# Row projections by halves of k with 512 moving columns, and split output projections

## The reference

```
h = rms_norm(x); a_u, a_v, a_g, b_q, b_k, b_v, b_g, m_q, m_g = split(h @ w_in)      # layer 0
...
h = rms_norm_2(x); q, k, v, g_ret, x_lru, y_lru, gate_ret, gate_lru = split(h @ w_in)   # layer 2
o = head_group_norm(retention(rotary(q), rotary(k), v))
y_a = (o * silu(g_ret)) @ w_ret_o
y_b = (rg_lru(conv(x_lru)) * gelu(y_lru)) @ w_lru_o
x = x + (sigmoid(gate_ret + b0) * y_a + sigmoid(gate_lru + b1) * y_b) @ w_out
h = rms_norm_2(x); gate, val = split(h @ ffn_w_up)
x = x + (gelu(conv(gate)) * val) @ ffn_w_down; return rms_norm_2(x)
```

## Time and profile before

| | us |
|---|---|
| median of 3 runs | 942.85 (942.73 to 944.76) |
| the profiled execution, its own time | 941.22 |
| its span, first to last instruction | 939.4 |

### The profile page before, as it was taken

How to read it: one execution, slowest core, us unless ns; L and a number is a source line. 1 busy time by engine, 2 the same in 40 slices (tenths; PEclk the granted TensorE clock), 3 DMA queues, 4 the chain that set the end, 5 groups by cost and what they waited for, 6 DMA issues and landing times.

```text
span 939.4 us, 15308 instructions
## 1 busy us (share of the span) xinstructions
PE 897.5 (96%) x6134; PEld 826.5 (88%) x6134; DVE 564.0 (60%) x1092; ACT 369.1 (39%) x682; POOL 103.3 (11%) x114
## 2 busy tenths in 40 slices
PE   6999998999999989999999999999999999999996
PEld 6998988888888777888999999998988999999995
DVE  4784687432979778712695478742423676666673
ACT  6556554111011244604344874552113344543451
POOL 0249650100011000202200000100000000000000
PEclk9999999999999899999999999999999999999999
DMA  9544314153443611220565263634513356645631
GB/s 366 189 146 136 115 65 171 54 182 132 154 161 119 241 46 46 105 91 22 206 222 179 90 214 133 219 108 179 180 52 128 136 180 201 207 168 188 223 136 45
DMA packets 37782, 139.36 MB, mean 148 GB/s; under 512 B 4304, under 2 KB 4432, under 8 KB 37456
## 3 DMA queue, kind: packets, MB, share of 16 engines
q1 hardware_dynamic: 37424, 136.90, 41.5%
q10 hardware_dynamic: 288, 1.48, 0.4%
HBM read 137.32 MB, written 1.05 MB: 147 GB/s over the span
## 4 chain that ended last, share of the span: by engine, by line
PE 79%; issue 8%; DVE 8%; ACT 3%; POOL 1%; DMA 1%; DVEq 0%; SPq 0%; ACTq 0%; POOLq 0%
PE psum L534 24%; PE psum L535 16%; PE psum L536 16%; PE psum L537 16%; PE psum L609 1%; PE psum L685 1%; PE psum L667 1%; ACT logits L1177 1%; DVE h_rows L1676 1%; PE psum L810 1%; PE psum L678 1%; DVE neg_max L1779 1%; DVE psum L1773 1%; POOL w_lo L2220 1%; DMA rows<-in_mem 1%
## 5 line engine op out<-in xcount | busy, mean ns | idle before, releaser
L534 PE MATMUL psum<-first 128*128 128x256 f32 (+1 forms) x960 | 216.3, 382 | 4.9 <-ACT first L1127 2.2
L1522 DVE TENSOR_TENSOR w_lo<-raw,w_hi 128x1024 fp32r<-128x1024 f32 x146 | 172.1, 1223 | 69.7 <-ACT w_hi L1089 68.8
L534 PEld LDWEIGHTS psum<-first 128*128 128x128 f32 x960 | 178.7, 192 | 30.4 <-ACT first L1127 2.8
L535 PE MATMUL psum<-h_hi,w_hi 128*128 128x256 f32 x704 | 199.7, 284 | 0.6 <-issue 0.6
L536 PE MATMUL psum<-h_lo,w_hi 128*128 128x256 f32 x704 | 199.2, 283 | 0.0
L537 PE MATMUL psum<-h_hi,w_lo 128*128 128x256 f32 x704 | 199.2, 283 | 0.0
L1089 ACT ACTIVATE w_hi<-raw 128x1024 fp32r<-128x1024 f32 x168 | 169.8, 1052 | 60.7 <-PE psum L537 37.4
L535 PEld LDWEIGHTS psum<-h_hi,w_hi 128*128 128x128 f32 x704 | 135.1, 192 | 1.6 <-issue 1.4
L536 PEld LDWEIGHTS psum<-h_lo,w_hi 128*128 128x128 f32 x704 | 135.1, 192 | 0.2
L537 PEld LDWEIGHTS psum<-h_hi,w_lo 128*128 128x128 f32 x704 | 135.1, 192 | 0.0
L535 PE MATMUL psum<-w_hi,h_hi 128*128 128x256 f32 x448 | 129.5, 289 | 0.0
(11 more groups left out here) (265 smaller groups left out, 1051.5 us busy)
## 6 DMA issues: line engine op xcount, KB each, us to landing
raw<-in_blocks SPq DMA_DIRECT2D x168, 512.0 KB, 4.2
first<-in_blocks SPq DMA_DIRECT2D x64, 512.0 KB, 4.4
w_late<-in_blocks SPq DMA_DIRECT2D x20, 512.0 KB, 4.5
early<-in_early SPq DMA_DIRECT2D x1, 1579.0 KB, 16.5
attention<-in_late ACTq DMA_DIRECT2D x1, 1376.0 KB, 5.6
rows<-in_mem SPq DMA_DIRECT2D x2, 512.0 KB, 4.5
x<-in_x SPq DMA_DIRECT2D x1, 1024.0 KB, 8.5
out_x<-h_rows SPq DMA_DIRECT2D x2, 512.0 KB, 2.6
```

The lines of the kernel that those rows point to most:

```text
L534: return nc.tensor.matmul(out, lhs[0], rhs[0], start=start, stop=stop, skip_group_check=shared_bank)
L535: nc.tensor.matmul(out, lhs[0], rhs[0], start=start, stop=False, skip_group_check=shared_bank)
L1522: V.tensor_tensor(split_part(w_lo, q), raw[:, q % RAW_SLOTS, :], split_part(w_hi, q).bitcast(F32), ALU.subtract).then_inc(w_lo_vector, 1)
```

## The change

Fourteen names are now in `WIDE`. A half of such a block is four k tiles with all 512 columns (the host lays the weights out that way), and `wide_piece` moves 512 columns per matmul: 24 matmuls a half, first the four k tiles for token tile 0, then for token tile 1. Each token tile has its own bank, so both banks are held over both halves, and they are filled at the end of the second half, the first 12 matmuls before the second. The first half's end has a semaphore of its own, `wide_half`. For the second bank `after` is set by `level(1)`, one half further than the usual. Readers of these banks now find 512 columns of one token tile. The recurrence's output projection (lru_o) and the mixer's (mix_out) leave `LATE_WHOLE` and become split products, lru_o in feature form, mix_out in wide form; their sources lru_y and mix0 to mix3 are split into y_t by ScalarE (`upper`) and VectorE (`lower`). In mix_out0's first half k goes outermost and each pair of k tiles waits for its own mix part. The first tanh of g_ret moves behind two retention heads. The squares of x3 are summed over 512 columns of one token tile.

```diff
@@ -93,10 +93,13 @@
 HALVES = (L0_SPLIT + both_of(["x_lru0", "x_lru1", "r_q", "r_k", "y_lru0", "y_lru1", "r_v0", "r_v1", "g_ret0", "g_ret1"]
-                 + MIX_ORDER[0:4] + ["ret_o0", "ret_o1"])
+                 + MIX_ORDER + ["mix_out0", "mix_out1"])
...
+
+WIDE = ["b_q", "b_k", "m_qg0", "b_v"] + L0_FILL + ["r_q", "r_k", "g_ret0", "g_ret1", "mix_out0", "mix_out1"]
@@ -116,13 +119,12 @@
-LATE_WHOLE = both_of(["lru_w", "lru_o0", "lru_o1", "mix_out0", "mix_out1"])
+LATE_WHOLE = both_of(["lru_w"])
...
-LATE_BESIDE = {("r_q", 0): (0, 1), ("g_ret1", 0): (2, 3), ("ret_o0", 1): (4,), ("ret_o1", 0): (5,), ("ret_o1", 1): (6, 7),
-               ("up_g0", 1): (8, 9)}
+LATE_BESIDE = {("r_q", 0): (0, 1)}
@@ -223,10 +225,16 @@
+def piece_end(p, layer):
+
+    name, t = FILL[layer][p]
+    return 2 * KT * (p // 2) + (KT + KT // 2, 2 * KT)[t] if name in WIDE else KT * (p + 1)
...
-    before = fill_after(i - 1, layer) // KT if i else 0
-    return range(before, fill_after(i, layer) // KT)
+    before = fill_after(i - 1, layer) if i else 0
+    return [p for p in range(len(FILL[layer])) if before < piece_end(p, layer) <= fill_after(i, layer)]
@@ -515,11 +526,12 @@
-            def level():
-
+            def level(further=0):
+
+                n = begun[0] + further
                 if begun[0] <= len(L0_SPLIT):
-                    return min(begun[0], len(L0_SPLIT) - LEAD) if begun[0] else -LEAD
-                return begun[0]
+                    return min(n, len(L0_SPLIT) - LEAD) if begun[0] else -LEAD
+                return n
@@ -572,9 +584,36 @@
+            def wide_piece(name, half, src, k_first=False, ready=lambda k: None):
+
+                begin((name, half))
+                w = half_view((name, half), CH)
+                n = KT // 2
+                order = [(t, k) for k in range(n) for t in range(T)] if k_first else [(t, k) for t in range(T) for k in range(n)]
+                for t, k in order:
+                    use = (name, t)
+                    if (half, k) == (0, 0):
+                        proj.claim(pe, use)
+                    if t == 0:
+                        ready(half * n + k)
+                    mm = products(psum[:, PROJ_BANK + proj.slot(use), :],
+                                  pick(src, slice(None), half * n + k, slice(t * P, (t + 1) * P)),
+                                  pick(w, slice(None), k, slice(None)), (half, k) == (0, 0), (half, k) == (1, n - 1))
+                    if (half, k) == (1, n - 1):
+                        fill(proj, mm, use)
+                        if t == 1:
+                            proj.after[use] = level(1)
+                            ends((name, half), *full_value(proj, use))
+                    elif (t, k) == (1, n - 1):
+                        wide_begun[0] += 1
+                        mm.then_inc(wide_half, 1)
+                        ends((name, half), wide_half, wide_begun[0])
+                    yield
...
                 for half in range(2):
-                    for _ in rows_piece(name, half, src, cols[half]):
+                    for _ in wide_piece(name, half, src) if name in WIDE else rows_piece(name, half, src, cols[half]):
@@ -936,13 +975,17 @@
+            def mixed(k):
+                if k % 2 == 0:
+                    src_lo.wait(pe, f"mix{k // 2}")
...
             for half in range(2):
-                for _ in rows_piece("g_ret0", half, h_t):
+                for _ in wide_piece("g_ret0", half, h_t):
@@ -957,16 +1000,16 @@
                 turn_pair(f"ret_y{j}", lambda a, t: h_rows[:, t, (2 * j + a) * P:(2 * j + a + 1) * P])
-            src_full.wait(pe, "lru_y")
-            project_features("lru_o0", lambda k: [tile_of(3072, k)])
-            project_features("lru_o1", lambda k: [tile_of(3072, k)])
+            src_lo.wait(pe, "lru_y")
+            project_features("lru_o0", y_t)
+            project_features("lru_o1", y_t)
...
             project_features("ret_o1", h_t)
-            src_full.wait(pe, "mix3")
-            mixed = lambda k, t: [tile_of(1024, k)[:, t * P:(t + 1) * P]]
-            project("mix_out0", mixed)
-            project("mix_out1", mixed)
+            for half in range(2):
+                for _ in wide_piece("mix_out0", half, y_t, half == 0, mixed):
+                    pass
+            project("mix_out1", y_t)
@@ -1154,7 +1197,11 @@
                 x_ready.wait(act, f"{name}_{c}")
-                for t in range(T):
+                if name == "x3":
+                    b, t = divmod(c, 2)
+                    ins = nc.scalar.activation(act_tmp[:, t, :], x[:, t, b * CH:(b + 1) * CH], ACT.Square,
+                                               accum_out=x_parts[:, t, b:b + 1])
+                for t in range(T if name == "x2" else 0):
@@ -1165,6 +1212,9 @@
                     arrive(proj, (name, half))
+                    if name in WIDE:
+                        proj.freed(nc.scalar.activation(dst[:, half, :], bank_of((name, half)), ACT.Copy), (name, half), act)
+                        continue
@@ -1394,18 +1444,18 @@
-            gate_tanh(0, 0)
...
                 if h == 2:
+                    gate_tanh(0, 0)
                     gate_tanh(0, 1)
-                    split_to(proj.after[("g_ret0", 1)] + LEAD + 1)
...
                 xpose.freed(ins, ("ret", h), act)
+            upper("lru_y", y_t[0][:, :, :].rearrange("p (t k) s -> p t (k s)", t=T), rows[:, :, 3072:4096])
@@ -1424,8 +1474,13 @@
                 source_hi(f"ret_y{j}", h_t[0][:, 2 * j:2 * j + 2, :], L("ret_gn")[:, 2 * j:2 * j + 2])
-            split_to(proj.after[("mix_out1", 1)] + LEAD)
+            for i in range(4):
+                split_to(proj.after[(f"lru_o{i // 2}", i % 2)] + LEAD)
+            for i in range(4):
+                split_to(proj.after[(f"ret_o{i // 2}", i % 2)] + LEAD)
+                upper(f"mix{i}", y_t[0][:, 2 * i:2 * i + 2, :].rearrange("p k s -> p (k s)"), pair_of(1024, i))
             for c in range(4):
+                split_to(proj.after[(f"mix_out{c // 2}", c % 2)] + LEAD)
@@ -2101,9 +2157,8 @@
                 vec.wait_ge(g_tanh, n + 1)
-                dst = rows[:, :, 2048 + 512 * b + HC * half:2048 + 512 * b + HC * (half + 1)]
-                proj.freed(V.scalar_tensor_tensor(dst, by_tokens(act_tmp[:, n % 2, :]), 1.0,
-                                                  by_tokens(bank_of(use)), ALU.add, ALU.mult), use, vec)
+                dst = rows[:, half, 2048 + CH * b:2048 + CH * (b + 1)]
+                proj.freed(V.scalar_tensor_tensor(dst, act_tmp[:, n % 2, :], 1.0, bank_of(use), ALU.add, ALU.mult), use, vec)
@@ -2130,6 +2185,13 @@
             normed.mark(V.tensor_tensor(h_rows[:, :, :], h_rows[:, :, :], rows[:, :, 2048:3072], ALU.mult), "g_ret", vec)
+            split_to(proj.after[("gate_r1", 0)] + LEAD)
+            src_hi.wait(vec, "lru_y")
+            for t in range(T):
+                at = (slice(None), slice(4 * t, 4 * t + 4), slice(None))
+                ins = V.tensor_tensor(y_t[1][at], rows[:, t, 3072:4096].rearrange("p (k s) -> p k s", k=4),
+                                      y_t[0][at].bitcast(F32), ALU.subtract)
+            src_lo.mark(ins, "lru_y", vec)
@@ -2141,12 +2203,14 @@
                             src_full.mark(V.tensor_tensor(part, part, pair_of(2048, i), ALU.add), f"mix{i}", vec)
+                            lower(f"mix{i}", y_t, (slice(None), slice(2 * i, 2 * i + 2), slice(None)),
+                                  part.rearrange("p (k s) -> p k s", k=2))
...
                     arrive(proj, use)
-                    part = x[:, :, b * CH + half * HC:b * CH + (half + 1) * HC]
-                    proj.freed(V.scalar_tensor_tensor(part, by_tokens(bank_of(use)), 0.5, part, ALU.mult, ALU.add),
+                    part = x[:, half, b * CH:(b + 1) * CH]
+                    proj.freed(V.scalar_tensor_tensor(part, bank_of(use), 0.5, part, ALU.mult, ALU.add),
@@ -2298,6 +2362,8 @@
             return tiles(w[h * HC:(h + 1) * HC])
+        if name in WIDE:
+            return tiles(w[h * CH:(h + 1) * CH])
```

More of the change, by code:

```diff
@@ L377, in build @@
         w_lo_vector = sem("w_lo_vector")
-        SRC = ([f"x0_{j}" for j in range(4)] + [f"x2_{j}" for j in range(4)] + [f"ret_y{j}" for j in range(4)]
-               + [f"x3_{j}" for j in range(4)] + [f"ffn{j}" for j in range(2 * FFN_STEPS)])
-        src_full = Milestones(sem("src_full"), ["cmp", "xc", "lru_y"] + [f"mix{i}" for i in range(4)]
+        MIXED = [f"mix{i}" for i in range(4)]
+        SRC = ([f"x0_{j}" for j in range(4)] + [f"x2_{j}" for j in range(4)] + ["lru_y"] + [f"ret_y{j}" for j in range(4)]
+               + MIXED + [f"x3_{j}" for j in range(4)] + [f"ffn{j}" for j in range(2 * FFN_STEPS)])
+        src_full = Milestones(sem("src_full"), ["cmp", "xc", "lru_y"] + MIXED
                               + [f"ffn{j}" for j in range(2 * FFN_STEPS)])
-        src_lo = Milestones(sem("src_lo"), [f"ffn{j}" for j in range(2 * FFN_STEPS)])
```

(14 more changed lines are left out.)

## The result

The changed kernel takes 947.6 us (median of 18 executions, 944.8 to 953.7), the kernel before 942.8 (18, 940.4 to 944.8): a ratio of 1.0063, 95% interval 1.0045 to 1.008. It is slower by 0.6%. The forecast was 936.9, faster.

What follows compares the result with a forecast made beforehand. TensorE, busy in 96% of the span, was taken as the bound; its work shrinks by 17.4 us, but stalls and clock falls leave a total of -5.9 us from 942.85, giving 936.9 us, forecast 934 to 940 (range 930 to 942).

Steps and rivals of the forecast that it cites:

- Steps of TensorE: Row projections: 512-column matmuls follow at 0.228 us, a half takes 5.47 us instead of 5.76, saving 0.29.
- lru_o: Recurrence's output projection: its four halves as split feature halves take 23.0 us, saving 4.6 us.
- the wait ahead of the mixer: From ret_o1 to mix_out0: TensorE's wait of 1.5 us shrinks to some 0.3, a gain of 1.2 us.
- mix_out and x3: Mixer projection to up_g0: 5.8 us saved, against 1.7 stall, 3.2 longer x3 chain and 1.2 clock; +0.3 without the earlier wait.
- Second bank emptied by ScalarE: end of pair + 0.2 + 2.0 (w_hi) + 0.6 (copy) = 2.9 us, 0.2 late: Where wide pair follows pair directly, b_k to m_qg0 and r_q to r_k: a loss of 0.25 us each.
- r_q and r_k: Second layer's row projections: 1.2 us saved by wide steps less 0.25 for a late second bank, -0.9 us.
- the entry: From b_q to the first scores: later norm chains outweigh 2.3 us of savings, +0.5 us, plus 1.2 for a clock fall.
- Of 8 x 0.29 = 2.3 us I keep 0.5: First layer's attention units: 0.5 us kept of the wide halves' saving, with bounds 2.3 and -2.
- The prediction's own sign: Attention units: the forecast is wrong if they gain or lose more than 2 us.
- rival 3: Attention units: bunched gelu pieces bring stalls and clock falls in four wide chunks, 12.8 us, 950 us in all; chance 0.06.
- Rival 4: Around g_ret and output halves: VectorE becomes the bound, 4.8 of 5.9 us go, 941 to 943 us; chance 0.13.
- The chances: Whole kernel: forecast range 0.62; faster, under 941.0, 0.84; within 0.09; slower 0.07.

Runs made afterwards that it cites:

- e2: Changed kernel with the split of one half more put behind emptying the second bank for mix_out0 and mix_out1 alone; 942.4 us, ratio to before 0.9998.
- e1: Changed kernel with the split of one half more put behind emptying a wide pair's second bank everywhere; 934.5 us, ratio to before 0.9909.
- e5: e1 with the second gelu pieces of a_v and a_u taken up one attention unit later; 931.6 us, ratio to before 0.9882.
- e9: e1 with the gelu polynomial's first step on VectorE reading one operand from PSUM; 929.2 us, ratio to before 0.9856.
- e3: Changed kernel with only mix_out wide, the split products kept and the split put behind emptying second banks; 931.3 us, ratio to before 0.9876.
- e6: e1 with the first layer's entry (b_q, b_k, m_qg0, b_v) wide but its four filler projections narrow; 933.8 us, ratio to before 0.9901.
- e8: e6 with the fillers a_g and b_g wide too, a_v and a_u still narrow; 933.5 us, ratio to before 0.9896.
- e4: e3 with r_q, r_k and g_ret wide too, the first layer still narrow; 930.15 us, ratio to before 0.9861.

## Why the prediction was wrong

- **Steps of TensorE: right.** Wide rows follow at 0.226 (704.23 to 705.36 above, five steps). The prediction lays its rows against a formula of the Trainium skill, page "TensorE: Matmul & The Clock Gate", section "Back-to-back issue gap", and leaves out what that section says of it: it is the gap of an isolated matmul, and a stream of weight loads and matmuls has some 131 ns at 512 columns. The trace is further from that (226 ns). lru_o fell by 4.3 for 4.6, the wait ahead of the mixer by 1.8 for 1.2, g_ret by 0.4 for 0.7.
- **mix_out and x3: right.** The stall of 1.7 us 12 matmuls in, w_lo ahead of the last update, the fall: +0.5 for +0.3. e2 shows the cause.
- **"Second bank emptied by ScalarE: end of pair + 0.2 + 2.0 (w_hi) + 0.6 (copy) = 2.9 us, 0.2 late": failed.** The sum has the w_hi pair run as soon as the weight slot is free. It left out the raw slot: its second quarter lands 4.2 us or more after VectorE has made the low parts of the quarter four before (4.6 to 5.7 in the traced cases), and VectorE was late by a convolution or a norm. 1.2 to 2.4 us in place of 0.25, at three places and not two, and one clock fall more. r_q and r_k came to +2.9 for -0.9, the entry to +2.7 for +0.5. e1 shows it: both stages then come out at or below the forecast. In the entry the prediction did follow a raw slot, but GpSimd's (a quarter landing at 73.6), and that one did not decide: a_u's w_hi pair began at 74.43, when TensorE had ended b_v, by then late by the two stops.
- **"Of 8 x 0.29 = 2.3 us I keep 0.5": failed by 6 us.** The prediction's own sign (the units gain or lose more than 2 us) came true. The step is the overlap: the gelu round trips and splits that were to stay covered hold back the probabilities, for 4.75 us once, and the clock falls. That is rival 3's mechanism, given 0.06; its price of 12.8 for four chunks was too high, its place right. That bunching is the reason is not shown (e5's units: 91.4). Mending the order takes the stalls of 2.3 and 4.9 us down to 2.0 and 2.7 and the clock fall behind the entry away, but brings others, and leaves the units at 91.6 (e1). e9 shows that 3.7 of the 5.3 us left there are VectorE's wait for GpSimd with its clock fall; the other 1.6 stay open. I had read GpSimd's row as a queue alone, never as something VectorE could wait for.
- **Rival 4, extra splits: not so.** e3 has them all and is 11.9 us faster than before.
- In sum: entry and units 7.2 over (8.4 for 1.2), r_q and r_k 3.8 over, the second layer 1.5 under (6.8 us of it at 1.2 GHz against 13.7 before): the 9.5 us between -5.9 and +3.6. The median is 2.9 above the profiled execution where before's was 1.6, for which the runs show only the lower clock; what sets its scatter stays open.
- **The chances.** The earlier trace rows were read as slack that the change would use. A stage in which TensorE waits for a round trip now and then had none here.

## What to carry to other kernels

When a buffer is released later or a half is prepared earlier, walk each engine's queue through every resource of the moved step (the weight slot, the raw slot and the load into it), and not only through the one that is named in the wait. If a step that frees a bank stands behind a step that only prepares, put it first: one line was worth 13 us here. A faster entry or wider step pays only as far as what meets it (a GpSimd row, a clock fall) stays where it was; so time parts of a change apart.

## What the runs showed of the hardware

- VectorE's TENSOR_SCALAR from SBUF to SBUF (128x512, 0.43 us alone) took 0.66 to 1.05 us in most cases beside GpSimd's low parts, but 2.6 us in e6 and e8 and 4.50 in e1 and e5, where it ended 0.3 us after GpSimd's row: it sat through four and seven GpSimd instructions of 0.73 us, the one under way included. What decides between one and seven stays open; the rows were unbroken in the short cases too. The SCALAR_TENSOR_TENSOR with one operand in PSUM took 0.69 beside the same row, as it does alone. The Trainium skill, page "SBUF — State Buffer", section "Who interferes with whom", says that a tensor_scalar in a 2-port mode and GpSimd exclude each other for a whole instruction, and that one SBUF input outside these modes does not contend. The trace agrees with both, save that the wait lasted for several instructions of the other engine; in which mode the tensor_scalar ran, it does not show.
- The clock falls move with the program, also where the code is the same: behind e6's wide entry the second layer was 3.5 us longer than e4's, and in after it is 1.5 us shorter than before's; in e2 r_q and r_k took 2.1 us more than in after (51.1 against 49.0), with 6.8 us at 1.2 GHz in place of 3.4. A difference of 2 us in a stage with waits can be no more than this.
